# Four small reorderings inside one streaming-encoder kernel: where TensorE waits for the attention inputs, when half of a weight split runs, when the last gate runs, and which queue loads a row of maxima

## The reference, cut to what matters

```python
hn = rmsnorm(x, norm_mix[l])
z = hn @ w_in[l] + b_in[l]
mq, mk, mv, mo, mi, mf, aq, ak, av = jnp.split(z, split_pts, axis=-1)
qk = jax.nn.silu(causal_conv(jnp.concatenate([mq, mk], axis=-1), conv_qk[l]))
...
hm = mlstm_chunkwise(...)          # chunks of the matrix memory
hm = hm * lax.rsqrt(jnp.mean(hm * hm, axis=-1, keepdims=True) + RMS_EPS)
hm = jax.nn.sigmoid(mo) * hm       # the output gate
ha = swa_sink_attention(...)
x = x + jnp.concatenate([hm, ha], axis=-1) @ w_out[l]
x = x + hier_moe(rmsnorm(x, norm_ffn[l]), ...)
return rmsnorm(x, norm_final)
```

## Time and profile before

| what | value |
|---|---|
| runs | 924.37, 927.26, 926.58 us; median 926.58 us |
| the profiled execution | 927.54 us, of which the span is 925.7 us |
| TensorE busy | 880.4 us (95%), 5134 matmuls |
| VectorE busy | 664.8 us (72%) |
| ScalarE busy | 451.6 us (49%) |
| GpSimd busy | 298.4 us (32%) |
| granted clock, mean | 0.979 |
| chain that ended last | PE 67%, DVE 10%, issue 7%, DMA 7%, ACT 3%, POOL 3% |

### The profile page before, as it was taken

How to read it: one execution, slowest core, us unless ns; L and a number is a source line. 1 busy time by engine, 2 the same in 40 slices (tenths; PEclk the granted TensorE clock), 3 DMA queues, 4 the chain that set the end, 5 groups by cost and what they waited for, 6 DMA issues and landing times.

```text
span 925.7 us, 16590 instructions
## 1 busy us (share of the span) xinstructions
PE 880.4 (95%) x5134; PEld 707.8 (76%) x5135; DVE 664.8 (72%) x1169; ACT 451.6 (49%) x716; POOL 298.4 (32%) x307
## 2 busy tenths in 40 slices
PE   8999999999999989999989999999999999999884
PEld 7888788988888868888777777877887676676662
DVE  7882357566575878888688888667646888888774
ACT  7432335343443525233234777555545676676662
POOL 0300000000000001100106887366335694786463
PEclk9999999999999999999978999999999999999998
DMA  8541103111110593321647999978886999999867
GB/s 309 134 114 46 46 24 102 36 57 58 33 58 14 181 309 108 109 103 71 248 182 228 345 377 373 327 220 279 266 248 214 344 338 324 319 337 354 272 197 296
DMA packets 89405, 185.18 MB, mean 200 GB/s; under 512 B 8495, under 2 KB 32420, under 8 KB 89350
## 3 DMA queue, kind: packets, MB, share of 16 engines
q1 hardware_dynamic: 79318, 155.07, 48.1%
q0 software_dynamic: 9872, 29.32, 12.0%
q10 hardware_dynamic: 160, 0.07, 0.0%
HBM read 152.46 MB, written 31.41 MB: 199 GB/s over the span
## 4 chain that ended last, share of the span: by engine, by line
PE 67%; DVE 10%; issue 7%; DMA 7%; ACT 3%; POOL 3%; SPq 1%; POOLq 1%; DVEq 0%; ACTq 0%
PE PS L2034 18%; PE PS L2038 17%; PE PS L2037 17%; PE PS L2363 2%; PE PS L2390 2%; DMA VM<-acc_dram 1%; DMA qT<-shift_dram 1%; DMA xn_dram<-xnb 1%; DMA XT<-in_x_dram 1%; DVE WP L613 1%; PE PS L2169 1%; DMA gt<-comb_dram,gix 1%; PE PS L2418 1%; PE PS L2043 1%; PE PS L2044 1%
## 5 line engine op out<-in xcount | busy, mean ns | idle before, releaser
L1757 DVE TENSOR_TENSOR WL<-RAW,WH 128x2048 fp32r<-128x2048 f32 x94 | 214.1, 2289 | 50.4 <-ACT WH L1099 50.1
L1099 ACT ACTIVATE WH<-RAW 128x2048 fp32r<-128x2048 f32 x96 | 183.7, 1914 | 26.0 <-PE PS L2038 17.8
L2034 PE MATMUL PS<-WH,XH 128*128 128x512 f32 x304 | 126.5, 416 | 2.2 <-ACT YB L1218 1.5
L2038 PE MATMUL PS<-WH,XL 128*128 128x512 f32 x304 | 119.4, 393 | 0.0
L2037 PE MATMUL PS<-WL,XH 128*128 128x512 f32 x304 | 118.9, 391 | 0.0
L838 POOL TENSOR_TENSOR dst<-dst,stat 128x4 f32<-128x4 f32 x8 | 8.3, 1039 | 328.9 <-DVE dst L1716 328.9
L846 POOL TENSOR_TENSOR stat<-stat 128x1 f32<-128x1 f32 x107 | 73.6, 699 | 48.9 <-ACT YB L1211 28.1
L2034 PE MATMUL PS<-HNH,WP 128*128 128x512 f32 x208 | 85.0, 409 | 1.6 <-issue 1.6
L2038 PE MATMUL PS<-HNH,WP 128*128 128x512 f32 x208 | 82.5, 397 | 0.0
L2037 PE MATMUL PS<-HNL,WP 128*128 128x512 f32 x208 | 82.4, 396 | 0.0
L2034 PEld LDWEIGHTS PS<-WH,XH 128*128 128x128 f32 x304 | 57.1, 188 | 22.6 <-issue 12.8
(11 more groups left out here) (416 smaller groups left out, 1922.5 us busy)
## 6 DMA issues: line engine op xcount, KB each, us to landing
RAW<-in_w_gate_dram SPq DMA_DIRECT2D x32, 1024.0 KB, 10.4
RAW<-in_w_up_dram SPq DMA_DIRECT2D x32, 1024.0 KB, 9.8
RAW<-in_w_down_dram SPq DMA_DIRECT2D x32, 1024.0 KB, 6.0
wraw<-in_w_in_dram SPq DMA_DIRECT2D x22, 512.0 KB, 4.0
XT<-in_x_dram SPq DMA_DIRECT2D x8, 512.0 KB, 6.8
vo_dram<-vo SPq DMA_DIRECT2D x16, 256.0 KB, 2.1
wout<-in_w_out_dram SPq DMA_DIRECT2D x4, 1024.0 KB, 6.8
VM<-vo_dram SPq DMA_DIRECT2D x16, 256.0 KB, 5.8
```

The source lines that it names most:

```text
L1099: A(WH[:, d % SPLITS, :], RAW[:, j, :], ACT.Copy).then_inc(s_whi, 1)
L1757: V.tensor_tensor(WLS[d % SPLITS][:, :], RAW[:, TURN[d][1] if d else 0, :], WH[:, d % SPLITS, :].bitcast(fp32), ALU.subtract).then_inc(s_w ...
L2034: first = mm(bank, ah, bh, start=start, stop=False)
L2038: return mm(bank, al, bh, start=False, stop=stop)
```

## The change

Four edits, none of which adds or removes arithmetic.

1. Seven waits of TensorE, among them the one for the last biased attention query (`biased(SLOT0 - 1)`), stand behind the job of slot 0 and no longer ahead of it.
2. `group_lo` in slots 5, 13 and 21 does the first half of the group only; the second half follows at the end of VectorE's next slot (6, 14, 22), behind the softmax.
3. `output_gate(7)`, three small additions for `fold` and the scaling of `wr` stand in chunk 1 and no longer in chunk 0. SP issues the last two loads of `wout` ahead of the stores of the last two gates.
4. `load_shift` moves from SP's queue to GpSimd's, one chunk of the loop ahead of GpSimd's power; it now waits for its predecessor's landing.

```diff
-        s_shift, SHIFT = (s_akdup, s_avdup), 32
+        s_shift, SHIFT = s_wr, 80
...
-        def load_shift(sp, s):
-            sp.wait_ge(s_pt, s - 1)
-            sp.wait_ge(s_qs, s - 1)
-            sp.dma_start(qT[:, :, P * (s - 2):P * (s - 1)],
+        def load_shift(pool, s):
+            pool.wait_ge(s_pt, s - 1)
+            pool.wait_ge(s_qs, s - 1)
+            pool.wait_ge(s_shift, SHIFT + 16 * (s - 2))
+            pool.dma_start(qT[:, :, P * (s - 2):P * (s - 1)],
                          bass.AP(shift_dram.tensor, shift_dram.offset + s * H * P, [[0, P], [P, H], [1, P]])
-                         ).then_inc(s_shift[s % 2], 16)
+                         ).then_inc(s_shift, 16)
...
-        def group_lo(dve, g):
-            for h in range(2):
+        def group_lo(dve, g, halves_=(0, 1)):
+            for h in halves_:
...
             load_o(0)
             load_o(1)
+            for k in range(0, 4, 2):
+                sp.dma_start(wout[:, k:k + 2, :], w_out_v[:, k:k + 2, :]).then_inc(s_wout, 16)
             for m in range(14, 16):
                 store_vo(sp, m)
-            for k in range(0, 4, 2):
-                sp.dma_start(wout[:, k:k + 2, :], w_out_v[:, k:k + 2, :]).then_inc(s_wout, 16)
...
-                if c + 2 < NT:
-                    load_shift(sp, c + 2)
...
+                if s + 2 < NT:
+                    if s == 0:
+                        pool.wait_ge(s_shst, SHST + 16)
+                    load_shift(pool, s + 2)
                 if s < NT:
                     pool.wait_ge(s_ms2, s + 1)
...
                 for g in split_after(n):
-                    group_lo(dve, g)
+                    group_lo(dve, g, (0,) if j % 4 == 1 else (0, 1))
...
+                    if j % 4 == 2:
+                        for g in split_after(n - 1):
+                            group_lo(dve, g, (1,))
...
                 if s == 0:
                     output_lo(1)
+                if s == 1:
                     output_gate(7)
...
-            pe.wait_ge(s_col, 3)
-            pe.wait_ge(*biased(SLOT0 - 1))
...
             for j in range(33):
                 if j < 32:
                     job(SLOT0 + j)
+                if j == 0:
+                    pe.wait_ge(s_col, 3)
+                    pe.wait_ge(*biased(SLOT0 - 1))
```

More of the change, by code:

```diff
@@ L1423, in exponents @@
                 else:
-                    dve.wait_ge(s_shift[s % 2], SHIFT + 16 * (s // 2))
+                    dve.wait_ge(s_shift, SHIFT + 16 * (s - 1))
                 for h in range(H):
@@ L2149, in _ @@
                     job(SLOT0 + j)
+                if j == 0:
+                    pe.wait_ge(s_col, 3)
+                    pe.wait_ge(*biased(SLOT0 - 1))
+                    pe.wait_ge(s_akdup, 32)
+                    pe.wait_ge(s_avdup, 32)
+                    pe.wait_ge(s_set, 2)
+                    pe.wait_ge(s_cols, 2)
+                    pe.wait_ge(s_rb, 1)
                 c = j // 2
```

## The result

| kernel | median (runs) | ratio to before, 95% interval |
|---|---|---|
| before, timed beside it | 926.12 us (7) | |
| changed | 931.33 us (7), 928.69 to 933.01 | 1.0059 [1.0045, 1.0074] |

What follows compares the result with a forecast made beforehand. TensorE, busy 95% of the span, was taken to bound the kernel. From the profiled execution, 927.54 - 1.5 + 3.5 - 1.1 - 1.7 = 926.8 us, written as a median of 926.5; range 922.8 to 930.2.

Steps and rivals of the forecast that it cites:

- What bounds the kernel: Whole kernel: TensorE, busy 95% of the span; an edit is worth what it changes in TensorE's idle time.
- edit 1: Slot 0: TensorE's 1.58 us gap goes, VectorE is late next, the transposes move by 1.47 us; bounds 0.34 and 1.58.
- Edit 2: Slots 7/8, 15/16, 23/24: gap shrinks 1.12 to 0.74, then late loads cost 1.18 each; +3.5 us, bounds 2.6 and 5.6.
- The rival that the split costs nothing: Slots 7, 15, 23: the second edit gains 0.38 us three times, nothing downstream late; sum 922.1 us, chance 0.18.
- Edits 3 and 4: Chunk 1: gate's 1.52 us hidden in VectorE's idle time, 2.04 wait for maxima gone; VectorE 2.4 us earlier at x2_half.
- the queue is no bound and I take the median: 345.7: Chunk 1: xr issued at 340.4; transfers from the gate's store end at 343.1, so xr lands after the median 5.3 us.
- The term for chunk 1: Chunk 1: waiting for xr leaves 1.1 of 2.4 us gained, so -1.1; at most 2.0 gained, or 6.2 lost.
- The longest landing: Chunk 1, a rival: xr takes its longest landing, 12.6 us, giving 934.1 us; chance 0.03.
- The clock: Stretch 350 to 354 us: with a wait of 0.9 instead of 1.66, the clock fall goes; -1.7 us, bounds 0 and 1.7.
- the rival that the fall isn't tied to the waits: Stretch at 350 us: the clock fall stays whatever the waits; 928.5 us, chance 0.12.
- the second rival: Slots 7 and 8, 15/16, 23/24: the clock falls, 1.7 us each; one in each place gives 932.0 us, chance 0.12.
- The sum: Whole kernel: 927.54 - 1.5 + 3.5 - 1.1 - 1.7 = 926.8 us, written as 926.5: no change.

Runs made afterwards that it cites:

- only_split: The kernel before with only the split of group_lo into two halves (second half behind the softmax); 931.04 us, ratio 1.0056.
- no_split: The changed kernel without the split of group_lo, its other three edits kept; 925.56 us, ratio 0.9991 to the kernel before.
- xr_first: no_split with the first load of xr issued ahead of the last gates' stores; 922.98 us, ratio 0.9960 to the kernel before.
- split_pts_first: only_split with ScalarE copying pts ahead of the high parts in slots 7, 15, 23 and 31; 930.36 us, ratio 1.0042 to the kernel before.

## Why the prediction was wrong

**What bounds the kernel, and edit 1**: right. 1.45 of 1.47 us.

**Edit 2**: the mechanism was right in each step (0.74; job 8 waits; the load goes out late; ScalarE idles behind a DMA of `wraw`; `pts` late), and the size was within its bounds of 2.6 to 5.6: 4.3 by the slots of `only_split` instead of 3.5, the difference in the two places where the load landed after 4.2 and 4.3 us instead of 3.8. The rival that the split costs nothing fell.

**Edits 3 and 4**: the 2.04 for the maxima went, and the gate's time was hidden, as forecast. The step that failed is the landing of `xr`: **"the queue is no bound and I take the median: 345.7"**. `xr` was to land 5.3 us after its issue; it took 9.4 here and 8.8 in `no_split`, and the wait was 3.33 (4.27) instead of 1.3. Three things were wrong in it.

The median of 5.3 is that of all eight loads of `xr`, six of them issued in later chunks, while this very load took 11.4 in the kernel before. I had counted 2.9 MB down to the first `xr`; but `nfb` and both loads of `xr`, issued within 2 us, were in flight together (`nfb` took 8.9, the first `xr` 9.4), and the maxima add 0.26: some 3.7 MB. And I had let them drain at the 387 GB/s of the earlier trace rows, a stretch in which all loads were long issued, while the two windows of `no_split` show 114 and 299 GB/s, that is 0.46 + 1.20 = 1.7 MB in the 8 us from 332 on, where the gate ended at 332.65. The other 2.0 MB take about 5 us more at the 387 GB/s of the earlier trace rows: an estimate of 345, and `xr` landed at 345.8.

The kernel before could have told most of it: from the end of its gate to the landing of `xr` it took 343.4 - 326.25 = 17.1 us, and without the 2.1 MB of `wout` at 387 GB/s 11.7 are left, as an estimate; the forecast had 345.7 - 335.7 = 10.0, and it became 13.2 in `no_split` and 13.7 in the changed kernel.

The term for chunk 1 was -1.1, and its place lost 2.6 us (2.0 in `no_split`, 32.1 against 30.1). `xr_first` shows the cause by taking `xr` out of that queue; why the burst is slow behind its first 0.7 us, the runs don't settle. The longest landing had been priced as a rival, with 0.03, since it came behind 2 MB of `wout`; the middle between 5.3 and 12.6 had no chance of its own, and there it fell.

**The clock**: this step failed as well. The forecast took away 1.7 us for the fall at 350, taking it that the shorter wait would end it. In the changed kernel the wait grew instead, and a fall of the same length followed it, at 355 to 359. The premise, that the fall is tied to the wait, is borne out: over the thirteen traces the clock fell at chunk 1's wait in six of the seven in which it was 1.66 us or more (the seventh had fallen in chunk 0), and in none of the six in which it was 0.91 or less; behind chunk 0's wait of about 1.75 it fell in four of thirteen. So the rival that the fall isn't tied to the waits has the traces against it, and with it the reading, by the rule alone, of the Trainium skill ("TensorE: Matmul & The Clock Gate", section "HAM oscillation"), which warns of gaps longer than any in these places of the kernel before: with a fall behind 1.66 in the kernel before, this trace does not agree that only longer gaps count. But the price was wrong: without the fall chunk 1 to chunk 2 is only 0.7 us shorter, since TensorE then waits 0.44 to 0.48 us for a low part that VectorE writes (`HTL`). Two more falls came in the slots, in two of the three places of the second rival, which had them at 1.7 each; they cost 0.9 where a wait for `pts` would have stood anyway and 1.6 where none would.

**The sum again**, in medians: edit 2 alone +5.2 (forecast +3.5), the other three -0.8 (forecast -1.5 - 1.1 - 1.7 = -4.3), together +4.4, measured +5.2, each with an interval of 1.3 to 1.4 each way. Of the miss of about 5 us, 1.7 is edit 2's size and 3.5 is `xr` and the clock. By place the two profiled executions give more, 6.5 + 2.6 - 1.5 = +7.6, of which 2.2 is by how much the slots took longer than in `only_split`, with two clock falls in them; how often the other executions had these falls is not shown. That the two profiled executions are only 3.5 apart is luck of the stretches without an edit: the fall at 76 to 82 us in the one before, and the 2.7 behind chunk 7, where its clock was at the lower level for 20.5 us from 473 us on against 13.7 in the changed kernel.

## What to carry to other kernels

Before work is moved behind a wait, list every DMA that its queue issues later, and look up how long that very load took in the trace before, even where nobody waited for it; a median over all loads of the tensor hides it. Then charge the first one needed with everything that is in flight with it. When a buffer can be loaded again only after it has been read, delaying half of the reading delays the next load, and with it everything that an in-order engine has queued behind that load. To bring a late result forward, look first for work ahead of it that nobody waits for, and follow that work to its next reader.

## What the hardware showed

The DMA engines were busy without moving much behind the opened gate: 159 GB/s at a share of 0.83 in the changed kernel, against 385 at 1.02 four us later. In `no_split` GpSimd's queue took 45.4% of the engines' time for 0.25 MB, SP's 29.2% for 0.40; yet without GpSimd's load the rate was as low, so its share is no proof that it costs the others. In `xr_first`, where `xr` is not in it, the same burst moved 141 GB/s at a share of 0.77 from 334 to 338 us. A 512 KB load in such a burst landed 8.6 to 9.4 us after issue; behind 2.1 MB of `wout` as well, it had taken 11.4 in the kernel before and 13.2 with edit 4 alone, where 4.4 and 5.3 were the least and the median of all eight before. The granted clock fell behind two waits of 0.74 and 1.02 us in slots 7/8 and 23/24 of the changed kernel, but not behind the same two in slots 15/16, nor in any of the six places of `only_split` and `split_pts_first`; a fall of 3.4 us cost 0.7, 0.9 or 1.6 us, by what else TensorE would have waited for. A load of the maxima issued by GpSimd took 0.78 to 0.81 us of its timeline against the 0.63 of the earlier trace rows.
